# Hybrid sparse-attention decoder step: cached blocks of the samples loaded by choice instead of by page

## What is computed

```
s = einsum('bqhgd,bnhd->bhgqn', qf, cmp_k)              # 64 compressed keys per sample and head
p_cmp = masked_softmax(s - m * dist, ...)
imp = sum(p_cmp over the 4 heads of a group), two compressed blocks per block of 64 positions
score = where(blk <= cur, where(forced, FORCE_SCORE, imp), NEG_INF)   # 33 blocks; first, last cached and new one forced
top_s, top_i = lax.top_k(score, 16)
k_sel, v_sel = sel_k[.., top_i], sel_v[.., top_i]       # 15 cached blocks and the new one
p_sel = masked_softmax(q . k_sel - m * dist, mask)
o_sel = p_sel . v_sel
```

## Time and profile before

| | |
|---|---|
| runs | 2675.2, 2677.11, 2685.92 us; median 2677.11 us |
| the profiled execution | 2676.88 us, of which its span is 2675.2 us |
| PE busy | 1895.4 us (71%) |
| DVE busy | 1095.8 us (41%) |
| POOL busy | 739.6 us (28%) |
| ACT busy | 439.3 us (16%) |
| moved by DMA | 911.81 MB, mean 341 GB/s over the span |

### The profile page before, as it was taken

How to read it: one execution, slowest core, us unless ns; L and a number is a source line. 1 busy time by engine, 2 the same in 40 slices (tenths; PEclk the granted TensorE clock), 3 DMA queues, 4 the chain that set the end, 5 groups by cost and what they waited for, 6 DMA issues and landing times.

```text
span 2675.2 us, 30528 instructions
## 1 busy us (share of the span) xinstructions
PE 1895.4 (71%) x11821; PEld 1225.1 (46%) x11821; DVE 1095.8 (41%) x1929; ACT 439.3 (16%) x978; POOL 739.6 (28%) x599
## 2 busy tenths in 40 slices
PE   5799999988889934677649897672764116565673
PEld 2477777868768934566536564121221101111120
DVE  2200002426583597676750127018777860000014
ACT  0100000122271212343400101110221000000011
POOL 1000000000010034443452223337546853222234
PEclk8899999999999976787769998766887556777785
DMA  9889997434047689999999999999999999999997
GB/s 385 288 312 347 330 330 239 143 96 156 11 142 233 204 307 416 411 413 412 413 421 402 418 417 417 414 402 405 390 381 410 379 390 406 401 414 421 422 421 315
DMA packets 283277, 911.81 MB, mean 341 GB/s; under 512 B 22254, under 2 KB 158498, under 8 KB 209978
## 3 DMA queue, kind: packets, MB, share of 16 engines
q0 software_dynamic: 78384, 569.78, 52.2%
q1 hardware_dynamic: 176354, 304.77, 32.0%
q10 hardware_dynamic: 28396, 35.35, 3.7%
HBM read 901.18 MB, written 17.21 MB: 343 GB/s over the span
## 4 chain that ended last, share of the span: by engine, by line
DMA 43%; PE 34%; DVE 12%; POOL 7%; issue 3%; ACT 1%; ACTq 0%; SPq 0%; DVEq 0%; POOLq 0%; PEldq 0%
DMA sb_ring<-in_peer_v_dram,sb_modT 19%; DMA sb_ring<-in_peer_u_dram,sb_dist 18%; PE ps L418 14%; POOL sb_ring L2650 7%; DVE sb_ring L2120 4%; PE ps L2572 3%; DMA sb_ring<-in_w_ada_dram 3%; PE ps L212 3%; PE ps L1873 2%; DMA sb_ring<-in_cache_sel_kv_dram 1%; PE ps L2328 1%; PE ps L2291 1%; PE ps L751 1%; PE ps L761 1%; DMA sb_pT<-in_cache_sel_kv_dram 1%
## 5 line engine op out<-in xcount | busy, mean ns | idle before, releaser
L2120 DVE SCALAR_TENSOR_TENSOR sb_ring<-sb_ring,sb_pT 128x2048 f32<-128x2048 f32 x264 | 602.6, 2294 | 244.2 <-DMA sb_ring<-in_peer_u_dram,sb_dist 199.7
L2650 POOL DMA_INDIRECT sb_ring<-in_peer_u_dram,sb_dist x256 | 423.4, 1654 | 532.7 <-DVE sb_ring L2120 352.3
L2572 PE MATMUL ps<-sb_ring,sb_xT 128*32 128x512 f32 x2048 | 343.5, 767 | 192.1 <-DMA sb_ring<-in_peer_v_dram,sb_modT 188.9
L2650 POOL DMA_INDIRECT sb_ring<-in_peer_v_dram,sb_modT x256 | 255.6, 998 | 561.5 <-PE ps L2572 543.7
L418 PE MATMUL ps<-sb_hT,sb_ring 128*128 128x264 f32 x1664 | 374.8, 388 | 0.0
L418 PEld LDWEIGHTS ps<-sb_hT,sb_ring 128*128 128x128 f32 x1664 | 315.5, 190 | 65.3 <-issue 13.0
L2572 PEld LDWEIGHTS ps<-sb_ring,sb_xT 128*32 128x32 f32 x2048 | 49.9, 121 | 426.3 <-DMA sb_ring<-in_peer_v_dram,sb_modT 381.0
L2407 PE MATMUL ps<-sb_ident,sb_ring 128*128 128x128 f32 x512 | 103.7, 359 | 135.9 <-DMA sb_ring<-in_cache_cmp_kv_dram 109.9
L1672 PE MATMUL ps<-sb_work,sb_pT 128*64 128x512 f32 x160 | 99.4, 708 | 98.0 <-ACT sb_work L1560 63.0
L2407 PEld LDWEIGHTS ps<-sb_ident,sb_ring 128*128 128x128 f32 x512 | 78.0, 184 | 159.4 <-DMA sb_ring<-in_cache_cmp_kv_dram 127.9
L2461 ACT ACTIVATE sb_pT<-ps 128x256 f32<-128x256 f32 x256 | 127.5, 661 | 97.0 <-PE ps L2407 96.8
(11 more groups left out here) (586 smaller groups left out, 2383.7 us busy)
## 6 DMA issues: line engine op xcount, KB each, us to landing
sb_ring<-in_w_ada_dram SPq DMA_DIRECT2D x48, 2048.0 KB, 11.1
sb_ring<-in_w_in_dram SPq DMA_DIRECT2D x26, 2048.0 KB, 14.3
sb_ring<-in_peer_wq_dram SPq DMA_DIRECT2D x19, 1024.0 KB, 13.3
sb_ring<-in_cache_cmp_kv_dram SPq DMA_DIRECT2D x68, 256.0 KB, 12.1
sb_ring<-in_w_out_dram SPq DMA_DIRECT2D x8, 2048.0 KB, 8.5
sb_ring<-in_cache_cmp_kv_dram ACTq DMA_DIRECT2D x60, 256.0 KB, 10.6
sb_ring<-in_w_out_dram SPq DMA_DIRECT2D x13, 1024.0 KB, 9.8
sb_pT<-in_peer_wq_dram SPq DMA_DIRECT2D x13, 1024.0 KB, 15.8
```

What stands on the lines that cost most here:

```text
L2120: dve.scalar_tensor_tensor(R3(rows), R3(rows), 1.0, h2r[t] if t < NT else R3(h2w), ALU.mult, ALU.mult, accum_out=(dots if t < NT else dots ...
L2572: mm = pe.matmul(bank(G % 2)[32 * q:32 * q + 32, :], w, rows[:, 512 * q:512 * q + 512], start=j == 0, stop=j == last)
L2650: pool.indirect_dma_start(rbuf[e % NBUF], None, io["peer_u" if kind == "u" else "peer_v"][0], bass.IndirectOffsetOnAxis(index, 0)).then_in ...
```

## The change

Only the 15 chosen cached blocks of each sample and head are loaded, keys and values alike. For that the ranking has to be known before the first block is fetched, so the compressed scores, their softmax, the ranking and a list of block numbers are made behind the last v steps of tile 0 instead of in tile 1's u steps.

- **Loads.** A block is one DMA of 32 KB (64 rows of 512 bytes). An item holds one sample, both heads: 30 DMAs, 16 by SP and 14 by ACT. There are 8 items of keys and 8 of values in place of 16 and 16. The 80 turns become 48, the selected columns 960 in place of 2,048.
- **Front.** `pe_samp_front` is advanced at v steps 110, 117 and 125 of tile 0, `act_samp_front` does the exponential, DVE's generator is advanced four times before tile 1's u steps. `pool_samp_keys` makes its constants before the gather of v step 116.
- **Block list.** DVE turns the ranking into a sorted list of 16 keys that hold position and physical block, splits it, and SP copies the 16 rows into one partition with 16 small DMAs before it may load the first block; SP and ACT read block numbers from there.
- **Behind the loads.** `SAMP_DOTS` goes from (26, 30, 38, 56, 76, 94, 100, 104) to (26, 34, 74, 78, 84). Behind dot 74 DVE waits for the scores of all keys. The values are taken every fifth v step of tile 1 instead of every seventh.

```
+        def load_picked(eng, i, blocks):
             half_free(eng, i)
+            kv, b = (0, i - 4) if i < 16 else (1, i - 16)
+            for h in range(KVH):
+                for s in blocks:
+                    at_ = 16 * (KVH * b + h) + s
+                    block_ = eng.value_load(block_row[0:1, at_:at_ + 1], min_val=0, max_val=2 * NPHYS - 1)
+                    eng.dma_start(half_slot[i % 3][SEL * (s % 2):SEL * (s % 2) + SEL, (8 * h + s // 2) * P:(8 * h + s // 2 + 1) * P],
+                                  sel_blocks[bass.ds(block_, 1), :, kv, h].rearrange("a t d -> (a t) d")).then_inc(half_in[i % 3], 16)
...
             for i in range(N_HALVES):
+                if i == 3:
+                    for b in range(NB):
+                        sp.dma_start(pages16[KVH * b:KVH * b + KVH], io["page_table"][b:b + 1, :].to_broadcast([KVH, PAGES])).then_inc(sem("pages16_in"), 16)
+                    sp.wait_ge(sem("blocks_ready"), 1)
+                    for p in range(PAIRS):
+                        sp.dma_start(block_row[0:1, 16 * p:16 * p + 16], picked_at[p:p + 1, :].bitcast(I32)).then_inc(sem("blocks_in"), 16)
+                    sp.wait_ge(sem("blocks_in"), 16 * PAIRS)
...
+            step(dve, c, dve.tensor_tensor(keys32, rank1[:, 0:NSEL - 1], block_key, ALU.mult))
+            step(dve, c, dve.max(out=keys16[:, 0:8], in_=keys32))
+            step(dve, c, dve.match_replace(out=keys32, in_to_replace=keys16[:, 0:8], in_values=keys32, imm_value=0.0))
+            step(dve, c, dve.max(out=keys16[:, 8:16], in_=keys32))
+            step(dve, c, dve.tensor_copy(I32v(key_int), keys16))
+            step(dve, sem("blocks_ready"), dve.tensor_scalar(I32v(picked_at), I32v(key_int), 1023, None, ALU.bitwise_and))
+            step(dve, c, dve.tensor_scalar(I32v(key_int), I32v(key_int), 10, None, ALU.logical_shift_right))
+            step(dve, sem("ranked"), dve.tensor_copy(back_of, I32v(key_int)))
...
             dve.wait_ge(sem("picked_mm"), 1)
...
+            for q, nb_ in enumerate((8, 7)):
+                dve.wait_ge(sem("chunk_mm"), q + 2)
...
-            for n in range(80):
+            for n in range(N_TURNS):
                 act.wait_ge(sem("kt_T"), n + 1)
...
+                if n == 7:
+                    act.wait_ge(sem("blocks_in"), 16 * PAIRS)
+                if n % 4 == 3 and 4 <= i < 12:
+                    load_picked(act, i, ACT_BLOCKS)
...
+        def pe_samp_front(pe):
...
+            pe.wait_ge(sem("pc_ready"), 1)
+            pe.matmul(bank(7)[0:PAIRS, 128:192], gsel, scmp, start=True, stop=True).then_inc(sem("imp_mm"), 1)
+            yield
+            pe.wait_ge(sem("ranked"), 1)
+            pe.matmul(bank(7)[0:ROWS, 192:192 + TOPN], gselT, back_of, start=True, stop=True).then_inc(sem("picked_mm"), 1)
...
-        REST_AT = [3 + 2 * i for i in range(47)]
+        REST_AT = [3 + 2 * i for i in range(46)] + [110, 117, 125]
-        SAMP_AT = [2 + 7 * i for i in range(8)] + [53] + [56 + i * 3 // 2 for i in range(HEADS)] + [68, 71]
+        SAMP_AT = [2 + 5 * i for i in range(8)] + [53] + [56 + i * 3 // 2 for i in range(HEADS)] + [68, 71]
-        SAMP_DOTS = (26, 30, 38, 56, 76, 94, 100, 104)
+        SAMP_DOTS = (26, 34, 74, 78, 84)
```

More of the change, by code:

```diff
@@ L29 @@
 PAST = 2048
+OLD = 15 * 64
 PAGES = PAST // P
@@ L1378, in layer_program @@
         half_in = [sem(f"half_in{j}") for j in range(3)]
[L1379 to L1382, removed]
+        N_HALVES, N_THIRD = 24, HEADS + KD
+        picked_item = lambda i: 4 <= i < 12 or 16 <= i < N_HALVES
+        half_count = lambda i: sum(16 * KVH * (TOPN - 1) if picked_item(k) else 16 for k in range(i % 3, i + 1, 3))
+        SP_BLOCKS, ACT_BLOCKS = range(0, TOPN - 1, 2), range(1, TOPN - 1, 2)
         def half_free(eng, i):
@@ L1387, in half_free @@
                 eng.wait_ge(sem("item_used"), i - 2)
[L1389 to L1395, removed]
-            half_free(eng, i)
[L1397 to L1401, removed]
+        sel_blocks = io["cache_sel_kv"][0].rearrange("n (u t) s h d -> (n u) t s h d", u=2)
+        def load_picked(eng, i, blocks):
+            half_free(eng, i)
+            kv, b = (0, i - 4) if i < 16 else (1, i - 16)
[5 more added lines that the diff above has]
+                                  sel_blocks[bass.ds(block_, 1), :, kv, h].rearrange("a t d -> (a t) d")).then_inc(half_in[i % 3], 16)
         def sp_samp(sp):
@@ L1407, in sp_samp @@
             for i in range(N_HALVES):
-                if paged(i):
-                    load_pages(sp, i, [pp for pp in range(8) if pp not in ACT_PAGES])
+                if i == 3:
[5 more added lines that the diff above has]
+                    sp.wait_ge(sem("blocks_in"), 16 * PAIRS)
+                if picked_item(i):
+                    load_picked(sp, i, SP_BLOCKS)
                 else:
@@ L1469, in dve_samp @@
             yield
[L1470 to L1477, removed]
             dve.wait_ge(sem("scmp_mm"), 1)
-            dve.wait_ge(sem("samp_consts"), 6)
+            dve.wait_ge(sem("samp_consts"), 4)
             step(dve, c, dve.tensor_tensor(gatesel.rearrange("p (r h) -> p r h", r=3), bank(7)[0:ROWS, 0:24].rearrange("p (h r) -> p r h", r=3),
@@ L1514, in dve_samp @@
+            step(dve, c, dve.memset(PTw3, 0.0))
+            for h in range(KVH):
+                step(dve, c, dve.memset(unfold[h], 0.0))
+                for g in range(4):
+                    mark(c, dve.tensor_copy(unfold[h][32 * g:32 * g + 8, 4 * h:4 * h + 4],
+                                            ident[32 * g:32 * g + 8, 32 * g + 4 * h:32 * g + 4 * h + 4]))
+            dve.wait_ge(c, n_static[c])
             yield
-            chunk(2)
+            dve.wait_ge(sem("samp_consts"), 10)
@@ L1679, in pe_samp @@
             i64 = ident[0:ROWS, 0:ROWS]
-            for k in range(PAGES):
-                mm = pe.transpose(bank(5 + k // 8)[:, (k % 8) * ROWS:(k % 8 + 1) * ROWS], ssel[:, k * P:(k + 1) * P], i64)
-                if k % 8 == 7:
-                    mm.then_inc(sem("samp_pT"), 1)
+            for k in range(8):
+                r = P if k < 7 else SEL
+                mm = pe.transpose(bank(5)[0:r, k * ROWS:(k + 1) * ROWS], ssel[:, k * P:k * P + r], i64)
+            mm.then_inc(sem("samp_pT"), 1)
             for k in range(4):
@@ L2218, in dve_window @@
             samp = dve_samp(dve)
-            next(samp)
+            for _ in range(4):
+                next(samp)
             dve.wait_ge(sem("spread"), 8)
```

153 lines of the change are left out of this document (83 added, 70 removed).

## The result

The changed kernel takes 2664.15 us (median of five runs, 2662.62 to 2666.32) against 2677.11 us before (five runs): ratio 0.9947, 95% interval 0.9933 to 0.9961. So 13 us are gained where 42 were forecast, and the time lies 0.15 us past the upper end of the range (2664), the end that took in rivals (a) and (c). The profiled execution took 2663.13 us, its span is 2661.4. It moved 894.06 MB, with 480 loads of 32 KB, as reckoned.

What follows compares the result with a forecast made beforehand. Full DMA engines were taken to bound tile 0's v steps and tile 1's u and v steps. Page loads removed, 100.4 us, less block loads added, 58, save 42; other terms 0: 2676.9 - 42 = 2635 us, range 2618 to 2664.

Steps and rivals of the forecast that it cites:

- (a): Tile 1's u steps: ACT's rounds take longer, DVE waits for late keys behind dot 74; 2651 to 2667 us; chance 0.14.
- (c): Tile 1's u steps: DVE and POOL set the pace, a hung gather dries up DMA; saving there lost, 2656 us; chance 0.12.
- The size of the saving: Both halves of tile 1: 256 page loads removed, 100.4 us, 480 block loads added, 58 us; 42 us saved.
- Rival (b): Both halves of tile 1: engines pay per load, not for bytes, so a block costs a page's price; 2765 us; chance 0.04.
- The front: Tile 0's v steps: scores, softmax, ranking and list moved there are covered by gathers and idle time; cost 0.
- SP's fits into it: Key loads: SP's 16 loads an item, 18 us, fit into ACT's round of 20.3 us.
- at about 2000: Tile 1's u steps: eight rounds from 1814, last issue 1971, SP's 1974, landed by 1995, last key scores at about 2000.
- The wait that was costed at 0: DVE behind dot 74, at 2015: no wait for key scores, 15 us to spare and another 15 of gathers under way.
- 13 us and not 21: Tile 1's v steps: half of the saving, about 21 us, was to come here, from the values' loads.
- What is late next: nothing: After the change: nothing replaces the removed transfers, since gathers alone have kept the DMA full.
- The hung gather: One gather hung behind DVE's longest sample block, costing DMA about 6 us; a shorter block may give 6 us back.

Runs made afterwards that it cites:

- e3: The changed kernel with DVE's sample work behind dots 94, 98, 104 and the values taken every seventh v step instead of every fifth: 2641.83 us.
- e6: e3 with SP's block loads alone, ACT's taken out, so 256 of the 480 block loads remain: 2631.52 us.
- e1: The changed kernel with DVE's sample work moved from dots 74, 78, 84 to dots 94, 98, 104: 2653.08 us.
- e11: The changed kernel with values taken every seventh v step instead of every fifth, DVE's dots left at 74, 78, 84: 2660.01 us.
- e2: The changed kernel with each load taking 32 rows of 1 KB instead of 64 of 512 bytes, half of each chosen block left out: 2654.94 us.
- e9: e3 with each block load cut to 32 of its 64 rows of 512 bytes, the other half of each block left out: 2615.32 us.

## Why the prediction was wrong

- **The size of the saving held.** With both waits out of the way (e3) the time is 34 us under before (27 to 42 by its interval); 42 were forecast. From 1840 to 1960 q1 and q10 took 15.0% of 120 us for 4.74 MB, 145 blocks: 0.124 us a block, 0.12 reckoned, packets of 25 ns. Rival (b) fell. It is a price for the two queues together: in e6, 224 of 480 loads taken away gave 10 us back, not some 27.
- **The front cost nothing**, as reckoned: 406 us for the v steps of tile 0 at the same DMA share. (Two readings there were loose and cost nothing: the 7.4 us of the earlier trace rows are the ranking without the softmax, and in the stretch from 1690, called gathers alone, 4.1% of the engines' time went to SP's queue, q1.)
- **The step that failed is "SP's fits into it" with the last scores "at about 2000".** SP's round was 24.6 us, not 18, and ACT's 23.4, not 20.3. The last load was issued at 2011 (1974), landed at 2035 (1995), and the scores were done at 2043. I took the price of a load from bursts of four, whose issues the trace before shows at 0.34 us, with pauses between them; in the change, where one item of 16 followed the other without a gap, SP took 1.62 us for a load of 80 packets. The wait that was costed at 0 was 24 us, with no more than 15 covered.
- **Rival (a)** named the right wait, on ACT; the traces show SP and ACT both, with SP ahead. At 24.6 us a round it would by its own reckoning have cost some 4 us ((24.6 - 20.3) x 8 less the 30 of cover). Taking the wait away gave 11 (e1), the values' spacing another 11 (e3); 7 of the 29 us between forecast and result are left, within e3's interval.
- **A step was missing.** Seven v steps became five between the values, and I never set an item's load time beside 15 us. That lay behind the first error: e1 shows it with 40 us of PE's waits, e3 leaves 8. It is part of why the v steps gave 13 us and not 21: in e11, without any wait for values, L2613 runs from 2203.8 to 2601.9, 398 us, in the change from 2202.0 to 2605.0, 403. The other 3 us stay open.
- **"What is late next: nothing" was wrong**: the scores, then the values. The hung gather stayed at 11.60 us; it left 7.5 us without work, some 6 before. Rival (c) fell as the main loss: the stretch from 2000 to 2050 is full once the wait is gone (e1).
- **A load kept SP longer than it kept the 16 DMA engines.** With its register read it took SP 1.2 us in the first two items and 1.62 from 1908 on, against 0.12 of all engines. I had made a rival of ACT's rounds and none of SP's.

## What to carry to other kernels

When small loads run beside a full stream, count packets as well as bytes: where two queues' packet counts are equal in a stretch (here 5,836 and 5,837) and the engine that issues the smaller packets is held (here issues of up to 2.1 us beside a median of 0.47), suspect that its queue goes at the pace of turns. Here 48 packets a load in place of 80, with the same bytes, took SP from 1.62 to 1.03 us a load (e2). Lay the loads' time of an item beside each place that asks for one, and move the askers to where the items can be. A wait taken out in one stretch may be the cover of the next, so test the edits alone and together.

## What was not expected

- The price of small packets is not a sum over loads: all loads of one of the two queues taken off, 224 of 480, gave 10 us (e6), while half of the rows taken off every load gave 26 (e9). Counts alone do not explain it: for each gather packet there were 1.00 small ones in e6 and 1.33 in e9 (8,415 of SP and ACT to 6,322 from 1840 to 1960), and still a gather packet took 0.303 us in e6 and 0.282 in e9. The cause stays open.
- A DMA share of 1.00 went with 271 GB/s (2285 to 2305 in the change) where no gather was issued for 19.75 us, up to 2302.18; with a mix of packets the share has to be read beside the bytes.
